# Chunked delta-rule scan: three products of a tile made once for both directions where the directions meet it in neighbouring chunks, with copies kept by ScalarE

## The reference

```python
kb = kc * bc[..., None]
a_low = jnp.where(strict, jnp.einsum('nbhcd,nbhsd->nbhcs', kb, kc) * decay, 0.0)
tmat = a_low + jnp.eye(C, dtype=f32)
...
qk = jnp.einsum('nbhcd,nbhsd->nbhcs', qc, kc) * decay
kd = kc * jnp.exp(g_last[..., None] - gc)[..., None]

def step(s, inp):
    w_i, u_i, qk_i, qg_i, kd_i, gl_i = inp
    v_new = u_i - jnp.einsum('bhcd,bhde->bhce', w_i, s)
    o = jnp.einsum('bhcd,bhde->bhce', qg_i, s) + jnp.einsum('bhcs,bhse->bhce', qk_i, v_new)
    s = s * jnp.exp(gl_i)[..., None, None] + jnp.einsum('bhcd,bhce->bhde', kd_i, v_new)
    return s, o
```

## Time and profile before

| quantity | value |
|---|---|
| median of 3 runs | 1705.09 us |
| lowest, highest | 1704.45, 1706.93 us |
| the profiled execution's own time | 1704.45 us |
| its span | 1702.3 us |
| mean granted TensorE clock | 0.983 |
| TensorE matmul busy | 95% |
| VectorE, ScalarE, GpSimd busy | 43%, 27%, 33% |

### The profile page before, as it was taken

One profiled execution on the slowest core, in us unless ns is written; L12 is line 12 of the kernel. 1 busy time (PEld: TensorE's weight loads), 2 busy tenths in 40 slices (PEclk: granted clock), 3 DMA queues, 4 the chain that ended last, 5 costly groups with the idle time before them and its releaser, 6 DMA issues. The chain is left out here.

```text
span 1702.3 us, 36038 instructions
## 1 busy us (share of the span) xinstructions
PE 1618.2 (95%) x14725; PEld 1108.7 (65%) x14725; DVE 734.4 (43%) x1515; ACT 466.6 (27%) x1042; POOL 569.8 (33%) x698
## 2 busy tenths in 40 slices
PE   6999999889999999999999999999979999999998
PEld 4577875557887865555556447786668986555544
DVE  4257543345545451121111546744456675224233
ACT  4212433253333131111111231253353322111111
POOL 2656304226566213111110155611538881000000
PEclk9999999999999989999999999999989999999999
DMA  9330100069884249999999302010220035899995
GB/s 337 91 115 26 50 15 28 13 191 289 253 269 176 75 176 338 372 359 360 357 342 344 110 25 75 25 50 17 63 85 24 15 124 209 336 413 407 411 413 227
DMA packets 160358, 323.73 MB, mean 190 GB/s; under 512 B 30153, under 2 KB 118127, under 8 KB 144879
## 3 DMA queue, kind: packets, MB, share of 16 engines
q1 hardware_dynamic: 127584, 287.20, 45.8%
q0 software_dynamic: 7008, 21.74, 4.6%
q10 hardware_dynamic: 25646, 13.12, 2.8%
HBM read 307.31 MB, written 14.71 MB: 189 GB/s over the span
## 5 line engine op out<-in xcount | busy, mean ns | idle before, releaser
L1531 PE MATMUL psum<-ring,arena 128*64 128x256 f32 x1536 | 172.8, 381 | 6.8 <-DVE arena L3131 3.4
L1531 PEld LDWEIGHTS psum<-ring,arena 128*64 128x64 f32 x1536 | 108.6, 137 | 68.3 <-issue 13.4
L3642 POOL DMA_INDIRECT big<-h_rows_lat,idx x16 | 15.7, 981 | 346.1 <-PE psum L1664 174.0
L802 PE MATMUL psum<-hT,ring 128*128 128x256 f32 (+2 forms) x496 | 130.2, 421 | 0.0
L3152 DVE TENSOR_TENSOR arena<-arena,psum 128x384 f32<-128x384 f32 (+1 forms) x32 | 15.6, 487 | 257.6 <-PE psum L1540 158.5
L802 PEld LDWEIGHTS psum<-hT,ring 128*128 128x128 f32 (+1 forms) x496 | 92.7, 188 | 36.9 <-issue 26.6
L3190 DVE SCALAR_TENSOR_TENSOR xT<-psum,modraw,xT 128x512 f32<-128x512 f32 (+1 forms) x136 | 79.7, 621 | 48.6 <-PE psum L1618 33.8
L975 PE MATMUL psum<-hT,ring 128*128 128x256 f32 (+1 forms) x192 | 80.0, 525 | 0.0
L2444 ACT COPY arena<-psum 128x512 f32<-128x512 f32 (+2 forms) x49 | 23.7, 483 | 202.5 <-PE psum L1553 143.4
L1614 PE MATMUL psum<-arena 128*128 128x512 f32 x144 | 65.8, 602 | 4.4 <-DVE arena L3177 2.7
L2754 DVE TENSOR_REDUCE small<-psum 128x1 f32<-128x768 f32 (+1 forms) x40 | 33.9, 849 | 82.3 <-PE psum L996 82.2
(11 more groups left out here) (476 smaller groups left out, 3771.7 us busy)
## 6 DMA issues: line engine op xcount, KB each, us to landing
ring<-in_moe_w_gate SPq DMA_DIRECT2D x64, 1024.0 KB, 9.6
ring<-in_ada_w SPq DMA_DIRECT2D x48, 1024.0 KB, 7.1
ring<-in_moe_w_up SPq DMA_DIRECT2D x32, 1024.0 KB, 10.3
hT<-in_moe_w_down SPq DMA_DIRECT2D x24, 1024.0 KB, 12.7
ring<-in_w_in SPq DMA_DIRECT2D x20, 1024.0 KB, 5.5
big<-in_moe_w_up SPq DMA_DIRECT2D x16, 1024.0 KB, 10.9
sz<-in_moe_w_down SPq DMA_DIRECT2D x16, 1024.0 KB, 12.5
big<-in_moe_w_down SPq DMA_DIRECT2D x16, 1024.0 KB
```

Of the source, the lines that this page charges most:

```text
L802: m = pe.matmul(b[0:c1 - c0, 0:n], lhsT=w[:, k, c0:c1], rhs=hT[:, k, t0:t0 + n], start=k == 0, stop=k == KD - 1)
L1531: m = pe.matmul(b[e * CAP_L:(e + 1) * CAP_L, 0:2 * P], lhsT=xs[:, k, e, 0:CAP_L], rhs=w[e][:, 2 * (k - ks[0]) + q, :], start=k == 0, stop= ...
```

## The change

A table `SHARED` lists, per layer, pieces (kind, chunk j) that are kept: layer 0 keeps `kr` and `qk` of chunk 0 and `kk` of chunk 3; layer 1 keeps `kr` of chunk 0 and `kk`, `kr`, `qk` of chunk 3. TensorE makes no product for the same kind in the next chunk. ScalarE copies the kept ones from PSUM into unused parts of `mixT`. VectorE reads the copy in both chunks, for direction 1 - d's tile in the second. Waits on the evacuation of these pieces go over to counts on `comb`. VectorE's operations stay the same in number and shape.

```diff
+SHARED = ((("kr", 0), ("qk", 0), ("kk", 3)), (("kr", 0), ("kk", 3), ("kr", 3), ("qk", 3)))
...
+        def kept(l, what, j, d):
+
+            i = tile_of(d, j)
+            row, col = 2, {"kr": (2, 5), "qk": (3, 4)}.get(what, (0, 1))[i] if i < CT else i
+            if i >= CT and what != "kk":
+                row, col = GH * (what == "qk"), i - CT - 1
+            return mixT[:, row:row + GH, col * P:(col + 1) * P]
+        def product_kept(l, what, j):
+            return (what, j) in SHARED[l]
+        def product_shared(l, what, j):
+            return (what, j - 1) in SHARED[l]
+        def factor_made(eng, l, what, j, d):
+            if product_kept(l, what, j) or product_shared(l, what, j):
+                base = sum(1 + IN_PAIRS + len(shared_steps(x)) for x in range(l)) + 1 + IN_PAIRS
+                eng.wait_ge(sems[l]["comb"], base + shared_steps(l).index((what, j, d)) + 1)
+            else:
+                evacuated(eng, (what, l, j, d))
...
# TensorE, gdn_piece
+                    if product_shared(l, what, j):
+                        return
...
# ScalarE, first in gdn_between(j, slot)
+                    for what, i, d in between(j, slot):
+                        if product_kept(l, what, i):
+                            if i == 3 and l == 0:
+                                for e in range(2):
+                                    factor_made(act, l, "qk", 1, e)
+                            b = product_ready(act, (what, l, i, d)).rearrange("p (h c) -> p h c", h=GH)
+                            read_out(act.copy(kept(l, what, i, d), b), (what, l, i, d))
...
# VectorE
+                def heads_product(what, j, d):
+                    if product_shared(l, what, j):
+                        return kept(l, what, j, d)
+                    if product_kept(l, what, j):
+                        evacuated(dve, (what, l, j, d))
+                        return kept(l, what, j, d)
+                    return product_ready(dve, (what, l, j, d)).rearrange("p (h c) -> p h c", h=GH)
...
-                        b = product_ready(dve, key).rearrange("p (h c) -> p h c", h=GH)
+                        b = heads_product(what, j, d)
```

More of the change, by code:

```diff
@@ L311, in tokens_made @@
         def tokens_made(eng, l):
-            eng.wait_ge(sems[l]["comb"], l * (1 + IN_PAIRS) + 1)
+            eng.wait_ge(sems[l]["comb"], sum(1 + IN_PAIRS + len(shared_steps(x)) for x in range(l)) + 1)
         def taps_added(eng, l, q):
-            eng.wait_ge(sems[l]["comb"], l * (1 + IN_PAIRS) + 2 + q)
+            eng.wait_ge(sems[l]["comb"], sum(1 + IN_PAIRS + len(shared_steps(x)) for x in range(l)) + 2 + q)
         def middle_taps(l):
@@ L541, in between, with shared_steps @@
             return out
+        def shared_steps(l):
+            order = [x for j in range(NT) for slot in range(len(BETWEEN)) for x in between(j, slot)]
+            return [(what, i, d) for what, i, d in order for w, j in SHARED[l] if what == w and i in (j, j + 1)]
+        def kept(l, what, j, d):
[14 more added lines that the diff above has]
+                evacuated(eng, (what, l, j, d))
         def ada_at(j, slot):
@@ L1084, in gdn_piece @@
                         evacuated(pe, ("v", l, j, d))
-                        evacuated(pe, ("qk", l, j, d))
+                        factor_made(pe, l, "qk", j, d)
                         for h in range(GH):
@@ L2774, in _, with factor_done @@
                 gX, gXC, gAO = lent_views(l)
+                def heads_product(what, j, d):
[5 more added lines that the diff above has]
+                    return product_ready(dve, (what, l, j, d)).rearrange("p (h c) -> p h c", h=GH)
+                def factor_done(ins, key):
+                    what, _, j, d = key
+                    if product_shared(l, what, j) or product_kept(l, what, j):
+                        ins.then_inc(s["comb"], 1)
+                    else:
+                        read_out(ins, key)
                 def gdn_piece(what, j, d):
@@ L2822, in gdn_piece @@
                         o = mixT[:, 2:2 + GH, i * P:(i + 1) * P]
+                        if j == 2:
+                            for e in range(2):
+                                factor_made(dve, l, "kr", 1, e)
+                        if j == 3:
+                            for e in range(2):
+                                factor_made(dve, l, "kk", 4, e)
                         first = [tile_of(1 - d, x) for x in range(NT)].index(i) > j
@@ L3420, in decays @@
                         if j:
-                            evacuated(pool, ("kk", l, j - 1, d))
+                            factor_made(pool, l, "kk", j - 1, d)
                         i = tile_of(d, j)
@@ L3447, in masks @@
                     for d in range(2):
-                        evacuated(pool, ("kk", l, j, d))
+                        factor_made(pool, l, "kk", j, d)
                     for n in range(FROM, LEVELS - 1):
```

18 lines of the change are left out of this document (9 added, 9 removed).

## The result

| | before | after |
|---|---|---|
| median us (runs) | 1706.21 (10) | 1715.62 (10) |
| lowest, highest | 1704.38, 1707.75 | 1709.51, 1719.55 |
| profiled execution, its span | 1704.45, 1702.3 | 1716.03, 1714.0 |
| its mean granted clock | 0.983 | 0.977 |

The ratio is 1.0054, 95% interval 1.0041 to 1.0067. The change costs 9.4 us, and the prediction (1703.6, range 1698.5 to 1709.0) is wrong: the time lies above the range, on the side that had a chance of 0.20.

A forecast was written before the change was run, and what follows sets the result against it. TensorE looked full in the scans' chunks, while layer 1's `level_factor` already waited for GpSimd. Layer 0's -2.3 and layer 1's -0.9 + 1.7 = +0.8 gave -1.5 us: 1702.95 profiled, 1703.6 as a median, range 1698.5 to 1709.

The forecast's parts named there:

- What is removed: TensorE in both scans loses 4.8 us of products in layer 0 and 5.75 in layer 1, together 10.6 us.
- layer 1's gain of nothing: Layer 1, chunks 3 and 4: TensorE's saving only adds 2 to 3 us to `level_factor`'s wait for GpSimd; gain 0.
- Rival (a): TensorE's time comes back as ScalarE's and GpSimd's chains shorten too: 6 to 10.6 us return, 1694.5 to 1699; chance 0.13.
- The 0.9 us of chunk 1: Layer 1, chunk 1: without `kr` ahead of z6 the chain to `v` comes 0.93 us earlier; gain 0.9.
- Layer 0, -2.3: Layer 0's scan: chunk 1 gains 1.5 us, chunk 3 gains 1.2, chunk 0 loses 0.4; sum -2.3 us.
- nothing on the DMA side: No DMA work is added; slot 4's block loads and the adaLN stores only go out up to 1.2 us later.
- ScalarE's copies at no cost: Fourteen bank copies, 0.58 us each, 8.1 in all; idle time takes them except in layer 0's chunk 0 (loss 0.4).
- VectorE's operands, +1.7 with an upper bound of 2.9: Layer 1's chain: moved operations with two SBUF inputs slow up to 1.54 times beside GpSimd; 1.7 us taken, 2.9 at most.
- Rival (b): VectorE and GpSimd obstruct each other in layer 1, which loses 6.3 us; kernel 4 us slower, 1709; chance 0.18.
- Rival (c), the clock: TensorE's new waits in layer 1's chunks 3 and 4 lower its clock, 1.6 us each time: 1705 to 1707; chance 0.09.
- Wrong if time changes outside the scans: Sign against the forecast: any change of time outside the two scans would show it wrong; no size given.

The follow-up runs named there:

- held_bank_psum: Changed kernel, but VectorE's kept and shared operations read one held PSUM bank, filled once (wrong values), instead of the copies; copies and waits stay: 1706.43 us, ratio 1.0006.
- made_again: Changed kernel, but TensorE makes the shared products again into a free bank that nobody reads: 1719.63 us, ratio 1.0087.
- layer0_only: The change in layer 0 alone, layer 1's scan as in the kernel before: 1705.85 us, ratio 1.0001.
- changed_filled: Changed kernel with small unread matmuls filling TensorE's gaps in layer 1's scan: 1712.52 us, ratio 1.0036.
- layer0_filled: The change in layer 0 alone, with small unread matmuls in layer 1's gaps of chunks 0, 1 and 3: 1703.84 us, ratio 0.9987.
- pair of held banks: Changed kernel with one PSUM bank held through the scan; VectorE reads that bank (1706.43 us) or the SBUF copies (1712.92 us).
- pair with fillers: Changed kernel and kernel before, each with small unread matmuls in TensorE's gaps of layer 1's scan: 1712.52 and 1704.25 us.
- kept_psum_filled: Changed kernel, VectorE reading PSUM in the chunk where the product is made, plus small unread matmuls in layer 1's gaps: 1707.05 us, ratio 1.0003.
- before_filled: Kernel before with small unread matmuls in TensorE's gaps of layer 1's chunks 0, 1 and 3: 1704.25 us, ratio 0.9987.
- before_filled_more: Kernel before with small unread matmuls in layer 1's gaps and 12 more in layer 0's chunk 0: 1707.64 us, ratio 1.0009.
- kept_psum_both: Changed kernel, but VectorE reads PSUM in the chunk where the product is made, the copy only in the next chunk: 1707.52 us, ratio 1.0004.

## Why the prediction was wrong, point by point

- **What is removed, and layer 1's gain of nothing: right.** TensorE's relief in chunks 3 and 4 turned into waits for GpSimd (5.6 and 3.6 us over layer 1 in `held_bank_psum`, after 2.9 and 1.6 before), and without contention the chunks stayed at 21.2. Rival (a) falls with it. The 0.9 us of chunk 1 is there once the clock is equal (16.9 against 17.7); in the change alone the chunk is 18.1, since it has more time at half clock.
- **Layer 0, -2.3: near in the scan of this profile, in part by luck, and not seen in the time.** Chunk 1 is 25.7 after 27.4, forecast -1.5; chunk 3 26.3 after 26.6, a gain of 0.3 where 1.2 was forecast; chunk 0 0.2 longer, forecast 0.4. That the sum comes to -2.7 is due to chunks 2 and 4, 0.5 and 0.3 shorter, of which nothing was forecast. `v` of chunk 1 starts at 410.36 behind 0.96 us of idle time, 0.5 us behind the start of the last L3602:

```profile
409.86 0.40 POOL L3602 COPY ring<-ring 64x256 f32<-64x256 f32 x1
```

  The eleven profiles with this part of the change average 162.6 us for the scan, the six without it 164.5: 1.9 us. One of the eleven is `made_again`, which has 163.1 with TensorE's work of before. But the two comparisons without fillers give ratios of 1.0001 and 1.0004, and that with equal fillers none. The profiles show one way in which the gain is lost. In `layer0_only`, `changed_filled` and `layer0_filled` chunk 1 takes 29.0 to 29.3 us, more than before. ScalarE's decays wait there 2.6 to 2.7 us for the DMA of their rows (1.2 before, 1.4 after), TensorE waits 2.3 to 2.4 us for ScalarE ahead of the last level, and 3.4 us at half clock follow. The forecast had put nothing on the DMA side. How often this happens in the timed runs is not shown, so this stays open; the intervals, of some 2 us either way, would still allow most of the gain.
- **ScalarE's copies at no cost: right by themselves.** They take 0.60 us each, forecast 0.58. VectorE waits 5.7 us for them in layer 1 of `held_bank_psum`, which loses nothing.
- **VectorE's operands, +1.7 with an upper bound of 2.9: the step that failed.** By the pair of held banks it is 6.5 us, and by the pair with fillers chunks 2 to 4 alone are 5.5 longer. Both the value and the bound were too low, for three reasons. First the price: I took 1.54 from the earlier trace rows as a rate at which a contended operation slows. What the rows after show is exclusion. The L2852 of chunk 2 starts at 1296.18, 0.08 us behind a GpSimd operation that ends at 1297.14, and ends itself at 1297.42, so 0.42 became 1.24:

```profile
1296.18 1.24 DVE L2852 TENSOR_TENSOR dT<-hT,arena 64x256 f32<-64x256 f32 x1
```

```profile
1296.10 1.04 POOL L3485 TENSOR_TENSOR arena<-arena,small 128x512 f32<-128x512 f32 x1 [0.30 <-ACT small L2254]
```

  In the other direction GpSimd's L3504 of 1328.63 began while VectorE's L2860 held it up and took 1.17 for 0.73. A short operation beside a long one so costs up to the rest of the long one, whatever its own length: 3 times its own time here. The Trainium skill says this, on a page that the prediction did not weigh (SBUF — State Buffer, SBUF: two separate sides): the pair of ports that VectorE and GpSimd share is an exclusive lock, held for a whole instruction, that a VectorE instruction with two SBUF inputs needs beside a GpSimd one that reads SBUF; the first to start gets it and the other fully blocks. The trace agrees by the ends above. The earlier trace rows did not contradict it: the operation of 0.96 us that took 1.48 began at 541.10, while one of GpSimd's ran to 541.76.
  Second the count: `kr` was not on my list for the binding chain, because it ran 1.65 us ahead of `kk`'s wait. At 3.13 for 1.29, and begun later behind ScalarE's copies, it used that slack up and set the start of `kk`. Third, GpSimd works through most of the chunk (18.36 of 23.79 us), and 9 of the 12 moved `kr` and `qk` operations of layer 1 met one of its instructions; against full contention I had held that its copies have one input, but those too made 0.28 and 0.42 us operations last 0.41 and 0.57.
- **Rival (b) was the mechanism, with its price too low.** It had 0.18, and gave 6.3 us for layer 1 and 1709 where 8.1 and 1715.6 came.
- **Rival (c), the clock: a small part.** The new wait of `v` in chunk 3 was followed by 3.52 us for it at half clock, as the earlier trace rows had shown for chunk 0. It costs little there, since `level_factor` waited for GpSimd even so (chunk 3 is 23.7 with the clock restored), and shows in chunks 0, 1 and 5 instead: 1 us by the runs with fillers, 2.7 by the profiles (8.1 less 5.4).
- **"Wrong if time changes outside the scans":** between them the profile after is 4.2 us longer, with 10.2 us more at half clock. This stretch varies from profile to profile (713.6 to 720.7 us) along with its half-clock time (10.2 to 23.9), whatever the kernel; `kept_psum_filled`, no slower than before, has the longest. Much of it is one place: in 11 of the 17 profiles the clock falls during or right behind the router's 16-column matmuls at about 575 us, and these have 17.1 us or more at half clock and take 717.2 to 720.7; the six without that fall have 13.7 or less and take 713.6 to 716.4. `before_filled` and `before_filled_more` are among the eleven. So I don't count it as the change's, but that it is none of it was not shown.
- **Sum.** Of the 9.4 us, 6.5 are the place of VectorE's operand (shown, to about 3 us), where the forecast had 1.7. `kept_psum_both`, which holds no bank, gets 8.1 back with half of the reads in PSUM, so it may be more; that kernel also frees its banks later, which was not taken apart. About 1 is clock that fillers give back to the change over what they give back to the kernel before (shown to within a few us only). The rest, some 2 us, is open.

None of the versions that keep shared products gains anything by it. `before_filled`, and `layer0_filled` with the same ratio, are 0.13% faster than the kernel before, with an interval that ends just under 1, and less than the 0.2% that a measurement tells apart for certain.

## What to carry to other kernels

Before moving an elementwise operand from PSUM to SBUF, ask whether the operation then has both inputs in SBUF and what GpSimd does at that moment; if it works, add the rest of its running instruction, not a percentage, and do so for every moved operation ahead of the chain's first shared wait, those with slack included. Work taken from a full TensorE is worth nothing where the wait behind it already ends on another engine; in this kernel the layer with no such wait gained in the scan of most profiles, if not in the time, and the other lost in both. And where a copy must be kept, let the first reader still read PSUM: that alone brought 8 of 9.4 us back.

## What the runs showed of the hardware

- VectorE's float32 operation of 128x512 with both inputs in SBUF takes 0.69 us alone (L2865 in layer 1's chunk 0, after), and 1.12 on average over the eight of layer 1, of which five met GpSimd's work, the longest taking 1.75; with one input in PSUM it takes 0.68. GpSimd's own 128x256 product goes from 0.73 to 1.17 us beside the copies' readers and stays at 0.72 beside an operation that reads PSUM. Moving the operand costs both engines. The wait stands inside the duration of the instruction, not as idle time before it.
- The granted clock can halve where the profile shows TensorE full (575 to 580 us after, 5.00 of 5.00 us busy at 0.50, during and behind 32 matmuls with outputs of 16 columns). The same place is at full clock in the profile before: 11 of 17 profiles have the fall there. Between the scans the time rises with the time at half clock, from 713.6 us with 10.2 to 720.7 with 23.9. Among 111 runs of the kernel before the mean clock goes along with somewhat under half of the variance in time (correlation -0.67).
- Fillers that took all half-clock time out of layer 0's scan raised the mean clock by 0.001 and made the kernel 3.4 us longer.
